# A gated-delta recurrence and its output product: block inversions dealt out anew between GpSimd and VectorE, some transfers moved to ScalarE's queue, and the product on split operands

## The reference

```
q, k, v, z, g, beta = gdn_project(...)          # for latent and context tokens
for d in range(N_DIRS):                         # forward and flipped
    oc, s_ctx = chunk_gated_delta(flip(qc), flip(kc), flip(vc), flip(gc[d]), flip(bc[d]), s0)
    ol, _     = chunk_gated_delta(flip(ql), flip(kl), flip(vl), flip(gl[d]), flip(bl[d]), s_ctx)
    o_lat = o_lat + flip(ol)
...
# in chunk_gated_delta, for each chunk:
lmat = a_low + eye                              # unit lower triangular
sol = triangular_solve(lmat, rhs, lower=True, unit_diagonal=True)
v_new = u_n - w_n @ S;  o_n = qd_n @ S + att_n @ v_new;  S = S * gt_n + kt_n^T @ v_new
...
# gdn_out
o = o * rsqrt(mean(o*o, -1) + eps) * o_gain * silu(z)
y = o.reshape(B, T, H*DV) @ w_out               # then h = x + gate_mix * y
```

## Time and profile before

| | |
|---|---|
| time of three runs | 2737.44, 2742.77, 2743.57 us; median 2742.77 |
| profiled execution | 2743.18 us; its span 2741.4 us |
| busy, share of the span | PE 85%, VectorE 37%, ScalarE 21%, GpSimd 10% |
| mean granted clock of TensorE | 0.924 |
| recurrence | about 400 to 737 us of the span |
| output stage | about 739 to 817 us |

### The profile page before, as it was taken

How to read it: one execution, slowest core, us unless ns; L and a number is a source line. 1 busy time by engine, 2 the same in 40 slices (tenths; PEclk the granted TensorE clock), 3 DMA queues, 4 the chain that set the end, 5 groups by cost and what they waited for, 6 DMA issues and landing times. The chain is left out here.

```text
span 2741.4 us, 29858 instructions
## 1 busy us (share of the span) xinstructions
PE 2335.7 (85%) x11740; PEld 1512.8 (55%) x11740; DVE 1005.3 (37%) x1774; ACT 577.4 (21%) x1217; POOL 264.3 (10%) x355
## 2 busy tenths in 40 slices
PE   4999986389886888888888888875998989799998
PEld 2877666389835333333333333332775767687776
DVE  3677426335625101101010110104653554464443
ACT  4442213044401100000000000002222421223311
POOL 4233335800000000000000000000000000000000
PEclk8999988599996899999999999997998999899999
DMA  6124627144311799999999999994321022221030
GB/s 215 58 83 134 219 92 203 36 136 119 131 47 61 295 417 417 418 418 417 416 416 417 418 417 418 418 416 156 128 89 34 31 100 77 98 92 62 31 131 31
DMA packets 209191, 569.88 MB, mean 208 GB/s; under 512 B 62553, under 2 KB 97346, under 8 KB 175682
## 3 DMA queue, kind: packets, MB, share of 16 engines
q1 hardware_dynamic: 206296, 559.97, 53.8%
q0 software_dynamic: 2496, 8.40, 1.0%
q10 hardware_dynamic: 297, 0.11, 0.0%
HBM read 540.14 MB, written 28.31 MB: 207 GB/s over the span
## 5 line engine op out<-in xcount | busy, mean ns | idle before, releaser
L1871 PE MATMUL ps_gate_up<-expert_ring_early,one_expert_columns 128*64 128x512 f32 x512 | 256.8, 660 | 87.7 <-DMA expert_ring_early<-in_moe_w_up_dram 73.9
L1871 PE MATMUL ps_gate_up<-expert_ring,one_expert_columns 128*64 128x512 f32 x512 | 235.3, 614 | 43.7 <-DMA expert_ring<-in_moe_w_up_dram 43.6
L1938 DVE TENSOR_TENSOR hidden_tokens<-silu_gate,ps_gate_up 64x512 f32<-64x512 f32 x64 | 42.4, 690 | 613.2 <-ACT silu_gate L1917 612.6
L1872 PE MATMUL ps_gate_up<-expert_ring_early,one_expert_columns 128*64 128x512 f32 x512 | 257.5, 661 | 0.0
L1872 PE MATMUL ps_gate_up<-expert_ring,one_expert_columns 128*64 128x512 f32 x512 | 236.0, 616 | 0.0
L1852 PE MATMUL ps_down<-expert_ring,hidden_columns 128*64 128x512 f32 x512 | 226.6, 595 | 0.0
L1851 PE MATMUL ps_down<-expert_ring,hidden_columns 128*64 128x512 f32 x512 | 226.6, 595 | 0.0
L1871 PEld LDWEIGHTS ps_gate_up<-expert_ring_early,one_expert_columns 128*64 128x64 f32 x512 | 74.8, 152 | 254.0 <-issue 254.0
L1871 PEld LDWEIGHTS ps_gate_up<-expert_ring,one_expert_columns 128*64 128x64 f32 x512 | 70.4, 141 | 190.5 <-issue 190.5
L1851 PEld LDWEIGHTS ps_down<-expert_ring,hidden_columns 128*64 128x64 f32 x512 | 67.5, 137 | 130.1 <-issue 127.9
L846 DVE SCALAR_TENSOR_TENSOR conv_out<-conv_in,tap_columns,conv_out 128x770 f32<-128x770 f32 (+1 forms) x96 | 122.3, 1274 | 3.4
(11 more groups left out here) (497 smaller groups left out, 4604.9 us busy)
## 6 DMA issues: line engine op xcount, KB each, us to landing
expert_ring<-in_moe_w_down_dram SPq DMA_DIRECT2D x64, 2048.0 KB, 19.0
expert_ring_early<-in_moe_w_gate_dram SPq DMA_DIRECT2D x32, 2048.0 KB, 16.0
expert_ring_early<-in_moe_w_up_dram SPq DMA_DIRECT2D x32, 2048.0 KB, 20.5
expert_ring<-in_moe_w_gate_dram SPq DMA_DIRECT2D x32, 2048.0 KB, 22.4
expert_ring<-in_moe_w_up_dram SPq DMA_DIRECT2D x32, 2048.0 KB, 24.2
win_ring<-in_gdn_w_in_dram SPq DMA_DIRECT2D x16, 1024.0 KB, 8.2
late_mod_ring<-in_w_mod_dram SPq DMA_DIRECT2D x16, 1024.0 KB, 5.5
stream_raw<-in_w_in_even_dram SPq DMA_DIRECT2D x16, 1024.0 KB, 5.2
```

The source lines that it names most:

```text
L1871: mm(psA[LO, c], xe[:, e, k], gu[s0][:, j, cols], start=(k == 0), stop=(k == KC - 1))
L1872: last = mm(psA[HI, c], xe[:, e, k], gu[s1][:, j, cols], start=(k == 0), stop=(k == KC - 1))
L1938: nc.vector.tensor_tensor(hid[HI, c % 2], sg[HI, c % 2], psA[HI, c], ALU.mult).then_inc(hidden, 1)
```

## The change

It has two parts. In the recurrence GpSimd inverts the context blocks of both directions in one pass on 128 partitions: the backward blocks are loaded into partitions of `El[0]` and copied, turned, beside the forward ones, so that one form of the row serves both, and in the results the parts of "inverse" and "turned inverse" are exchanged for the backward half. GpSimd then does only the backward latent blocks. VectorE does the forward latent ones after its pieces, and takes in the first three merges after rows 14, 23 and 30. ScalarE issues the eight context block loads, between its tenth and its eleventh decay, and, after its last decay, the backward direction's context stores and the loads of its first tile. SyncE loads v and k of the first tile after the first inputs.

In the output the two blocks become one. The weights come in four loads of 1 MB; ScalarE rounds them and the columns of o to a high part, GpSimd (weights) and VectorE (columns) subtract it to get the low part, and `split_product` (line 117) makes three matmuls on these for each fp32 one. The function `add_product` goes. The residual is loaded once the columns are turned.

```
+            def scatter(queue, u, d):
+                if u == 0:
+                    part = slice(d * UNIT_P[0], (d + 1) * UNIT_P[0])
+                    W, T = (Xc[part], Ec[part]) if d == 0 else (Ec[part], Xc[part])
+                    queue.wait_ge(inverted[0, 0], 1)
+                else:
+                    W, T = Xl[d][:, :, :], El[d][:, :, :]
+                    queue.wait_ge(inverted[1, d], 1)
+                queue.dma_start(W_dram[u][d], W.rearrange("p a b -> p (a b)")).then_inc(scattered[u, d], 16)
+                queue.dma_start(T_dram[u][d], T.rearrange("p a b -> p (a b)")).then_inc(scattered[u, d], 16)
...
@@ sync
-                store(range(0, LAT0))
-                for d in DIRS:
-                    blocks(0, d, LAT0)
+                store(range(0, len(PIECES)))
+                for d in DIRS:
+                    blocks(d)
+                scatter(sp, 0, 0)
+                inputs(sp, 0, 0)
                 for d in DIRS:
                     load_v(0, d)
                     load_k(0, d)
-                store(range(LAT0, len(PIECES)))
-                for d in DIRS:
-                    blocks(1, d, len(PIECES))
-                scatter(0, 0)
-                inputs(0, 0)
-                scatter(0, 1)
-                inputs(0, 1)
-                inputs(1, 0)
+                inputs(sp, 1, 0)
...
@@ scalar
-                for i in range(len(PIECES)):
+                for i in range(LAT0 + 2):
                     decay(i)
+                for i in range(AB):
+                    act.wait_ge(a_stored[i], 16 * len(range(i, LAT0, AB)))
+                for d, E, p0 in ((0, Ec, 0), (1, El[0], UNIT_P[0])):
+                    for b in range(BLOCKS):
+                        src = A_dram[d][span(b), 0:CT, :, span(b)].rearrange("j t h i -> (t h) j i")
+                        act.dma_start(E[p0 + b * CT * HEADS:p0 + (b + 1) * CT * HEADS], src).then_inc(e_loaded[0, d], 16)
+                for i in range(LAT0 + 2, len(PIECES)):
+                    decay(i)
+                scatter(act, 0, 1)
+                inputs(act, 0, 1)
@@ gpsimd
-                h1 = slice(UNIT_P[0], 2 * UNIT_P[0])
-                for u, d, inv in ((0, 1, BlockInverse(Ec[h1], Xc[h1], tmp[1][h1], True)),
-                                  (1, 0, BlockInverse(El[0][:, :, :], Xl[0][:, :, :], tmp[1][:, :], False)),
-                                  (1, 1, BlockInverse(El[1][:, :, :], Xl[1][:, :, :], tmp[1][:, :], True))):
...
+                back = slice(UNIT_P[0], 2 * UNIT_P[0])
+                ctx_inv = BlockInverse(Ec[:, :, :], Xc[:, :, :], tmp[1][:, :], False)
+                lat_inv = BlockInverse(El[1][:, :, :], Xl[1][:, :, :], tmp[1][:, :], True)
...
+                for d in DIRS:
+                    pool.wait_ge(e_loaded[0, d], 16 * BLOCKS)
+                nc.gpsimd.tensor_copy(Ec[back], El[0][back].rearrange("p a b -> p b a")).then_inc(ctx_turned, 1)
+                pool.wait_ge(ctx_turned, 1)
+                for j in range(ROWS):
+                    ctx_inv.row(nc.gpsimd, seq, j)
+                ctx_inv.turn(nc.gpsimd).then_inc(inverted[0, 0], 1)
+                pool.wait_ge(inverted[0, 0], 1)
+                pool.wait_ge(e_loaded[1, 1], 16 * BLOCKS)
+                for j in range(ROWS):
+                    lat_inv.row(nc.gpsimd, seq, j)
+                lat_inv.turn(nc.gpsimd).then_inc(inverted[1, 1], 1)
@@ vector
+                lat_inv = BlockInverse(El[0][:, :, :], Xl[0][:, :, :], tmp[0][:, :], False)
+                MERGED_AFTER = {14: 0, 23: 1, 30: 2}
...
-                dve.wait_ge(e_loaded[0, 0], 16 * BLOCKS)
+                dve.wait_ge(e_loaded[1, 0], 16 * BLOCKS)
                 for j in range(ROWS):
-                    ctx_inv.row(nc.vector, seq, j)
-                ctx_inv.turn(nc.vector).then_inc(inverted[0, 0], 1)
-                merged(0)
-                merged(1)
-                merged(2)
+                    lat_inv.row(nc.vector, seq, j)
+                    if j in MERGED_AFTER:
+                        merged(MERGED_AFTER[j])
+                lat_inv.turn(nc.vector).then_inc(inverted[1, 0], 1)
@@ gdn_output, scalar
+                weights_high(0)
+                weights_high(1)
+                keep_row(0, "gate_mix")
+                for k in range(HEADS):
+                    act.wait_ge(kept, k + 1)
+                    nc.scalar.activation(sh[:, k].bitcast(F32R), szT[:, k], ACT.Copy).then_inc(s_high, 1)
+                weights_high(2)
+                weights_high(3)
+                keep_row(1, "gate_ffn")
@@ gdn_output, gpsimd
+                for i in range(HALVES):
+                    pool.wait_ge(w_high, i + 1)
+                    nc.gpsimd.tensor_tensor(wl[:, i].bitcast(F32R), raw[:, i], wh[:, i], ALU.subtract).then_inc(w_low, 1)
@@ gdn_output, vector
+                for k in range(HEADS + 1):
+                    if k < HEADS:
+                        dve.wait_ge(turned, k + 1)
+                        nc.vector.scalar_tensor_tensor(out=szT[:, k], in0=ps[:, k % 2], scalar=gain, in1=szT[:, k],
+                                                       op0=ALU.mult, op1=ALU.mult).then_inc(kept, 1)
+                    if k:
+                        dve.wait_ge(s_high, k)
+                        take_low(nc, sl[:, k - 1], szT[:, k - 1], sh[:, k - 1]).then_inc(s_low, 1)
@@ gdn_output, tensor
+                for n in range(2 * LT):
+                    i, t = n // LT, n % LT
+                    if i:
+                        pe.wait_ge(taken, t + 1)
+                    for k in range(KC):
+                        if t == 0 and k % HK == 0:
+                            pe.wait_ge(w_low, 2 * i + k // HK + 1)
+                        if n == 0:
+                            pe.wait_ge(s_low, k + 1)
+                        half = 2 * i + k // HK
+                        last = split_product(nc, psD[:, t], [x[:, k, t * P:(t + 1) * P] for x in (sh, sl)],
+                                             [x[:, half, k % HK] for x in (wh, wl)], k == 0, k == KC - 1)
+                    last.then_inc(done, 1)
```

More of the change, by code:

```diff
@@ L1013, in inputs @@
[L1013 to L1034, removed]
@@ L1068, in _ @@
                     if g > 0 and g + 2 < NT:
[L1069 removed]
+                        inputs(sp, g + 2, 0)
                     load_k(g + 1, 0)
                     if g == 0:
[L1072 to L1073 removed]
+                        scatter(sp, 1, 0)
+                        inputs(sp, 2, 0)
                     load_k(g + 1, 1)
@@ L1522, in _, with rows @@
                 dve.wait_ge(z_loaded, 16)
-                for h in range(HEADS):
-                    dve.wait_ge(turned, h + 1)
-                    nc.vector.scalar_tensor_tensor(out=szT[:, h], in0=ps[:, h % 2], scalar=gain, in1=szT[:, h],
-                                                   op0=ALU.mult, op1=ALU.mult).then_inc(kept, 1)
+                for k in range(HEADS + 1):
[6 more added lines that the diff above has]
+                        take_low(nc, sl[:, k - 1], szT[:, k - 1], sh[:, k - 1]).then_inc(s_low, 1)
+                dve.wait_ge(h_loaded, 16)
+                dve.wait_ge(row_kept, 1)
+                for n in range(2 * LT):
+                    i, t = n // LT, n % LT
+                    cols = slice(i * COLS, (i + 1) * COLS)
+                    dve.wait_ge(done, n + 1)
+                    if n >= 2:
+                        dve.wait_ge(taken, n - 1)
+                    nc.vector.tensor_tensor(tmp[:, n % 2], psD[:, t], per["gate_mix"][:, cols], ALU.mult).then_inc(gated, 1)
+                    dve.wait_ge(gated, n + 1)
+                    nc.vector.tensor_tensor(h[:, t, cols], h[:, t, cols], tmp[:, n % 2], ALU.add).then_inc(taken, 1)
             @block.tensor
             def _(pe):
-                for g, part in ((0, 2), (1, 5)):
-                    if g:
-                        pe.wait_ge(row_kept, g)
+                def rows(g, part):
                     for k in range(KC):
@@ L1538, in _ @@
                     last.then_inc(row_done, 1)
+                rows(0, 2)
                 pe.wait_ge(normed, LT)
-                for h in range(HEADS):
-                    if h >= 2:
-                        pe.wait_ge(kept, h - 1)
+                for k in range(HEADS):
+                    if k >= 2:
+                        pe.wait_ge(kept, k - 1)
                     for t in range(LT):
-                        last = nc.tensor.transpose(ps[:, h % 2, t * P:(t + 1) * P], O[:, t, h], per["ident"])
+                        last = nc.tensor.transpose(ps[:, k % 2, t * P:(t + 1) * P], O[:, t, k], per["ident"])
@@ new lines, in _ @@
+                pe.wait_ge(row_kept, 1)
+                rows(1, 5)
+                for n in range(2 * LT):
+                    i, t = n // LT, n % LT
+                    if i:
[9 more added lines that the diff above has]
+                    last.then_inc(done, 1)
```

157 lines of the change are left out of this document (67 added, 90 removed).

## The result

| | kernel before | kernel after |
|---|---|---|
| median | 2743.17 us (4 runs) | 2709.33 us (4 runs) |
| ratio | | 0.987, 95% interval 0.9839 to 0.9901 |
| profiled execution, span | 2743.18, 2741.4 us | 2709.7, 2707.9 us |

The forecast was 2721.2 us, the time is 33.8 us under before and not 22. Of after's four times three lie within 0.4 us of each other and one is 2696.96. Before ran faster in every later comparison: 2738.01 (11 runs), 2734.53 (17) and 2735.96 us (9), where after stood at 2708.83 and 2710.97. Their ratios are 0.9898 (0.9882 to 0.9913) and 0.991 (0.9895 to 0.9924), 25 to 29 us less.

A forecast was written before the change was run, and what follows sets the result against it. PE was taken to be bound by its 52.67 us wait for inverted context blocks, then by the output product. 22 us from the recurrence and 0 from the output, off 2743.18, gave 2721.2 us, range 2709 to 2734.

The forecast's parts named there:

- Where the blocks come free: Start of the context inversion: both directions' inverted blocks ready at 473.3, 30.9 us before SyncE stores them now.
- Sharing of transfers: First tile's stores and loads on SyncE and ScalarE side by side: 2 us added between blocks and PE, bounds 0 and 5.
- VectorE's late merges: First merges of the recurrence: nine rows at 1.43 us delay the second merge, costing 6.6 us of the 28.9.
- rival 1: VectorE's latent rows not slowed, 0.88 us each; second merge 1.6 us late, 5.0 us more gain; chance 0.12.
- The stop of 8.39 us: Piece stage: VectorE's stop for an attention store mostly goes away, leaving SyncE free at about 470.
- The clock: PE's clock in the recurrence rises at the same place of the chain; otherwise about 3 us more won.
- The fourth merge: Recurrence: fourth merge at 524.9 in place of 547.22, 22.3 us earlier.
- Sum 0: Output product: 12 us less from three split products per fp32 one, given back at its start; bounds -12 and +5.
- PE's second row product fits ahead of that: Output stage start: PE's second gate row product, 3.78 us, is done before VectorE's column blocks end at 770.9.
- 22 + 0: Whole forecast: 22 us gained in the recurrence, 0 in the output product, giving 2721.2 us.
- rival 3: Output product keeps its 12 us, since GpSimd does not hold VectorE so long; 2709 us; chance 0.06.
- The likeliest case: The forecast itself, 2721.2 us, with its own range of 2716 to 2729 us; chance 0.62.

The follow-up runs named there:

- the recurrence alone: The kernel after's recurrence with the output stage of the kernel before; 2715.06 us, 0.9919 of before.
- the kernel with VectorE's low parts: Kernel after with both gate rows made early, VectorE taking the first two low parts, and the first tile's products between transposes; 2703.85 us, 0.988 of before.

## Why the prediction was wrong

- **Where the blocks come free: right in kind, 2 us too late.** The failing term is "ScalarE has to finish its tenth decay first (422.87 + 1.15 = 424.0)". I had the loads begin at 424.0, they began at 421.91, 1.0 us before the end of that decay (422.91). In all ten profiles in which ScalarE issues them it is 1.0 us. What they stand behind is the store of the last context piece: they follow its issue by 2.2 us in all ten, and in before SyncE's followed it by 2.1. The other 1.1 us is the piece stage: its ninth piece came 15.1 us behind the first where before had 16.2. That is not the change, for both lengths turn up in one kernel (after 15.1 and 16.3, before 16.2 and 15.2). The 8.3 us from the first issue to GpSimd's copy, the copy of 1.99 and the 37.1 us of rows on 128 partitions (432.29 to 469.40) are as forecast.
- **Sharing of transfers: 2 us put in, 1.0 measured** (16.8 against 15.8 us from store to merge).
- **VectorE's late merges: the right step, 1.5 us too dear.** Nine rows took 13.0 us, the 1.43 a row of the forecast, and the second merge was 15.53 - 9.03 = 6.5 us late, as said. But the four merges cost 32.16 - 27.08 = 5.1 us. PE has another product of the same merge (L1124, 2.07 us) to do anyway, so in before its next one starts 1.90 us behind VectorE's instruction; here that work was long done and it started 0.47 us behind. That rival 1's 0.88 a row holds without GpSimd, and only then, was shown by making GpSimd wait. VectorE had its fifteen rows done at 480.8 (forecast 485 to 488) and stood 7.34 us ahead of the first merge, by 1.43 us a row (an estimate) room for some five of the nine; no run here puts them there.
- **The stop of 8.39 us: gone, as said,** for the most part since the tile loads moved. SyncE's block loads were out at 464.8 and not at 470, which changes nothing: the context blocks were ready at 471.3.
- **The clock: as said.** Behind the fourth merge it was 0.50 for 12.7 us, in before for 12.8, and the way from there to the output took 191.8 us in both.
- **The fourth merge: forecast 22.3 us earlier, measured 26.9.** The 4.6 us between them are 2.0 to the store, 1.1 from there to the first merge and 1.5 to the fourth. Some 1.5 belong to the base, 1.1 of them the piece stage above: before's profile took 113.6 us from first piece to first merge, the two others with its recurrence 112.1 and 112.0. That leaves 25.6 us on average where I had 22.3.
- **The output product: "Sum 0" was 3 us short.** The subtraction did stretch the normalization (8.93), and the second did hold the first low part (2.23). Two terms behind it failed. The pace is 1.26 us a column block, where I had added two durations and gaps to 1.47; eight are 1.7 us. And the wait was another: "PE's second row product fits ahead of that" is wrong. PE ended its transposes at 738.4, did the second gate row until 741.8, and the product stood behind that; with both rows made early it started 26.0 us into the stage. The first product stands 29.4 us into it (forecast 31.4), and a triple takes 0.69.
- **The base.** I set the sum against 2743.18 us, and the median of the three times, 2742.77, agreed. The later medians of before are 5 to 9 us lower. The profile has 962.6 us in the experts, 959.1 to 959.7 in all the others, before's own second one among them: some 3 us that left with the comparison and were no gain of the change.

So 22 + 0 should have been 25.6 + 3.1 = 28.7 by the stages. By the times the recurrence alone is 23 us, and the output 6 (on top of it) or 11 (alone), so the sum is better known than its two parts; where the output's surplus over 3.1 comes from stays open. None of the rivals came about; rival 3 had the right sign for the output, at a quarter of its size. The first product's gain, 32.1 us, lies beyond the 28 to 30 that was to show the forecast right. The likeliest case's own range, 2716 to 2729, missed the time; the wide one, 2709 to 2734, held it by 0.3 us, which is luck: of after's later medians one, 2708.83, lies under it.

## What to carry over

Where two engines share work of the same kind, ask if it can lie behind each other: VectorE's rows took 0.42 us alone and 0.75 beside GpSimd's, and holding back GpSimd's rows for 39 us, which nobody needed yet, won 5 us of merges. A term of a forecast that is "duration plus gaps" deserves one row of the same pattern in the trace; mine was 0.2 us a step too high. Ask too what an engine's queue really waits for: the issue here did not wait for the end of the instruction ahead of it. And before a number is set down against one profile, compare a stage that the change leaves alone in a second one.

## What the runs showed of the hardware

- An untouched stage of the same matmuls took 95.3 us at a granted clock of 0.71 and 91.3 at 0.75 in two executions of one kernel. So one profile of each can't tell a difference of 4 us in the total.
- GpSimd subtracting 128x2048 held one VectorE addition of 128x512 for 3.45 us (0.69 alone), 4.77 in the kernel with VectorE's low parts; nobody waited there. GpSimd copies of 128x1024 (1.89 and 1.93 us) held a VectorE update for 1.94 and 1.96 us.
- ScalarE issued DMAs 1.0 us before the end of the activation ahead of them in its order, in ten profiles of ten.
- Loads issued by SyncE and ScalarE at the same time took 0.45 and 0.47 us an issue, SyncE's as alone. A store that ScalarE issued beside SyncE's took 1.18 us in all nine profiles with both, and 0.60 from SyncE alone.
